# GLA's decay chain one head ahead, modulation summed by block transposes, and a phase's first projection made in the phase before

## The chip, the cores and the metric

One core of a Trainium2 chip runs the whole kernel. The metric is the device time of one execution in microseconds, as a median of several runs. Engine names: PE is the matrix engine (TensorE), PEld its weight loads, DVE the vector engine, ACT the scalar engine, POOL the GpSimd engine, SP the sync engine, which here only starts DMAs. Each engine works through its own program in order; semaphores join them.

## The reference

One inference step of a two-layer streaming encoder on 512 prompt frames and 64 sample frames of width 1024. Layer 0 runs mLSTM and retention heads side by side, layer 1 gated linear attention (GLA) and gated DeltaNet. Input and output of a layer are modulated by vectors made from a condition c (adaLN): `silu(c) @ w_ada + b_ada`, a sum over 1024 rows. Cut to what the change touches:

```python
log_a = jax.nn.log_sigmoid(a1.astype(F32) @ w_a2 + b_a2) / C_TAU       # GLA: decay input, rank 16
b = jnp.cumsum(_to_chunks(log_a, cs), axis=3)
q_t = qc * jnp.exp(b)
k_t = kc * jnp.exp(-b)
s = jnp.where(causal, jnp.einsum('nbhtd,nbhsd->nbhts', q_t, k_t), 0.0)
S = a_c[..., None] * S + jnp.einsum('bhsd,bhsv->bhdv', k_c, v_c)       # state, chunk by chunk
o = jnp.concatenate([_head_rmsnorm(hc), _head_rmsnorm(hd)], axis=-1) * g_head
```

## The kernel before

The phases follow one another, each a block of five engine programs that ends with a barrier: mLSTM, retention, output of layer 0, GLA, DeltaNet, output of layer 1. The function `heads(nc, M, IN, OUT, kind)` (from line 839) builds the first three of the four head phases: kind A is mLSTM, B retention, C GLA, each with H = 4 heads. Activations stay on chip transposed as a high and a low half of float32 (`hT_high`, `hT_low`); each product of a projection is three matmuls (`split_matmul`, lines 180 to 182).

A head (`turn(h, ...)` on each engine) has two parts. First the q and k projections: CT tiles of weights (4 in A and B, 2 in C), each in two halves of 288 tokens into PSUM banks 0 and 1, 24 matmuls a half, 48 a tile. ACT copies each half out (line 1204). Then five blocks t: four of 128 prompt tokens and one of 64 sample tokens. Per block PE makes the gates' projection into bank 2 (`project_gates`) and v's into bank 3 (`project_v`), 24 matmuls each, the scores and a transpose of k (bank 4), the products of scores and state with v (bank 6), the state update (banks 0 and 1), and transposes the gated result of the block before (`turn_g`, line 1080, bank 7), which DVE puts into `gT` (line 1481). In block 0 the gates come first, then v (in mLSTM v after the scores). ACT in block 0 does the tanh of the gates (1241), then the copy of v (1247) on which PE's product with the scores waits, then the copy of that product (1253).

The last block's `turn_g` of a head is done in the next head: in A and B behind the first weight tile, in C at once, behind the decay products. At the end of a phase it stands alone and everything waits for it.

Weights come by SP's DMAs, 512 KB a tile, into rings of two (`rqk`, `rv`); ACT rounds each to its high half (960, 973) and DVE makes the low half (967, 979). The first two q/k tiles of retention and GLA, and all four tiles of DeltaNet's first head, are loaded and split in the phase before (`FirstLoads`); the rest of such a head is requested when the phase begins.

GLA's decay chain stands at the head's start: PE multiplies the rank-16 input by `w_a2` (1092) into banks 0 and 1, ACT adds the bias (1198), DVE and ACT compute log-sigmoid (188 to 196), DVE scales and scans it (1357, 1360), takes the middle and end of each block (1366 to 1368), shifts (1371), ACT makes the exponentials (1208 to 1210) that multiply q and k (1375, 1379). PE's first q product waits for bank 0, that is for ACT's line 1198.

`LaterModulation` uses DVE's spare time in mLSTM and retention: `dve_step` k = 0 to 7 accumulates `w_ada` rows times silu(c) for two conditions (m) into `acc` [128, 2, 512] (line 667, two instructions a step), one step each in blocks 0 to 3 and four before them. Then `pe_total` (677), inside the `turn_g` of block 3, sums over the 128 partitions with eight matmuls against ones, and `dve_take` (689) copies eight columns.

## Time and profile before

| | us |
|---|---|
| median of 3 runs | 1641.48 |
| lowest, highest | 1640.67, 1643.29 |
| the profiled execution | 1638.62 |
| its span, first to last instruction | 1636.80 |
| mean granted clock of PE in it | 0.971 of full speed |

In a row of the timeline the bracket is the idle time of that engine just before the instruction, and what ended it. The granted clock (PEclk) is 1.00 at 2.4 GHz and 0.50 at 1.2 GHz; a stretch with 0.75 spent half its time at the lower level. The drawn end of a matmul is modelled and lies behind the time at which PE can take the next.

### The profile page before, as it was taken

The page shows a single profiled execution, that of the slowest core. Times are in us where ns is not written, and L with a number is a line of the kernel's source. Part 1 is how long each engine was busy: PE and PEld are TensorE (multiplying, and loading weights), DVE is VectorE, ACT ScalarE, POOL GpSimd, SP SyncE. Part 2 cuts the span into 40 slices and gives each one's busy share as a digit, 9 for nine tenths or more (in the row PEclk, how much of TensorE's full clock was granted, in tenths as well). Part 3 has the DMA queues.
Part 4 walks back from the last instruction along what each step waited for, and adds up shares of the span by engine and source line. Part 5 has one row for each costly group of instructions (what it writes and reads, how often), then busy time and mean ns, then how long its engine had stood idle before and what let it go on. Part 6 is the DMA issues. An engine that isn't in the chain of part 4 may idle for free. (4 is left out here: it accounts for less than half of the span.)

```text
span 1636.8 us, 30957 instructions
## 1 busy us (share of the span) xinstructions
PE 1529.1 (93%) x11168; PEld 1428.5 (87%) x11168; DVE 961.2 (59%) x2118; ACT 628.2 (38%) x1491; POOL 181.9 (11%) x384
## 2 busy tenths in 40 slices
PE   6999999998999999899799999899999999977898
PEld 2689898987999999899698889899999999966898
DVE  2575555554766667633566645576677667753522
ACT  2522222222232222423544433254555465543521
POOL 1000000000000000001000010023123222312000
PEclk8999999999999999999899999999999999988899
DMA  9434343432552433123343213221211211020223
GB/s 328 116 102 115 86 110 89 114 86 49 126 154 70 118 95 109 61 96 100 103 85 85 63 33 80 73 69 45 58 45 48 60 43 54 5 73 3 89 88 116
DMA packets 195257, 140.89 MB, mean 86 GB/s; under 512 B 18332, under 2 KB 178584, under 8 KB 194916
## 3 DMA queue, kind: packets, MB, share of 16 engines
q1 hardware_dynamic: 177772, 130.16, 28.2%
q10 hardware_dynamic: 17400, 9.60, 2.0%
q8 instruction: 53, 0.87, 0.2%
q14 instruction: 32, 0.26, 0.1%
HBM read 128.58 MB, written 11.15 MB: 85 GB/s over the span
## 5 line engine op out<-in xcount | busy, mean ns | idle before, releaser
L180 PE MATMUL bank<-hT,w_high 128*128 128x288 f32 x1152 | 363.0, 315 | 6.2 <-ACT gla_ls_x L1198 2.4
L182 PE MATMUL bank<-hT,w_high 128*128 128x288 f32 x1152 | 344.2, 299 | 0.0
L181 PE MATMUL bank<-hT,w_low 128*128 128x288 f32 x1152 | 344.2, 299 | 0.0
L180 PEld LDWEIGHTS bank<-hT,w_high 128*128 128x128 f32 x1152 | 222.1, 193 | 8.6 <-ACT gla_ls_x L1198 2.6
L181 PEld LDWEIGHTS bank<-hT,w_low 128*128 128x128 f32 x1152 | 222.0, 193 | 0.0
L182 PEld LDWEIGHTS bank<-hT,w_high 128*128 128x128 f32 x1152 | 221.2, 192 | 0.0
L180 PE MATMUL bank<-output_w_split,gT_high 128*128 128x256 f32 x512 | 143.4, 280 | 0.0
L182 PE MATMUL bank<-output_w_split,gT_high 128*128 128x256 f32 x512 | 143.2, 280 | 0.0
L181 PE MATMUL bank<-output_w_split,gT_low 128*128 128x256 f32 x512 | 142.5, 278 | 0.0
L181 PEld LDWEIGHTS bank<-output_w_split,gT_low 128*128 128x128 f32 x512 | 96.8, 189 | 0.0
L180 PEld LDWEIGHTS bank<-output_w_split,gT_high 128*128 128x128 f32 x512 | 96.1, 188 | 0.1
L182 PEld LDWEIGHTS bank<-output_w_split,gT_high 128*128 128x128 f32 x512 | 95.9, 187 | 0.0
L180 PE MATMUL bank<-mlstm_w_v_low,hT 128*128 128x512 f32 (+1 forms) x256 | 88.8, 347 | 0.0
L181 PE MATMUL bank<-mlstm_w_v_high,hT 128*128 128x512 f32 (+1 forms) x256 | 86.2, 337 | 0.0
L182 PE MATMUL bank<-mlstm_w_v_high,hT 128*128 128x512 f32 (+1 forms) x256 | 85.6, 334 | 0.0
L180 PE MATMUL bank<-gla_w_v_low,hT 128*128 128x256 f32 x256 | 74.0, 289 | 0.0
L180 PE MATMUL bank<-retention_w_v_low,hT 128*128 128x256 f32 x256 | 73.5, 287 | 0.0
L181 PE MATMUL bank<-gla_w_v_high,hT 128*128 128x256 f32 x256 | 71.5, 279 | 0.0
L182 PE MATMUL bank<-gla_w_v_high,hT 128*128 128x256 f32 x256 | 71.4, 279 | 0.0
L182 PE MATMUL bank<-retention_w_v_high,hT 128*128 128x256 f32 x256 | 71.4, 279 | 0.0
L181 PE MATMUL bank<-retention_w_v_high,hT 128*128 128x256 f32 x256 | 71.4, 279 | 0.0
L2123 POOL TENSOR_TENSOR gdn_A_level<-gdn_AT,const 128x128 f32<-128x128 f32 (+1 forms) x120 | 61.0, 542 | 76.7 <-DVE gdn_AT L2038 68.1
(487 smaller groups left out, 3594.4 us busy)
## 6 DMA issues: line engine op xcount, KB each, us to landing
x<-in_w_in_even SPq DMA_DIRECT2D x72, 512.0 KB, 5.0
x<-in_w_in_odd SPq DMA_DIRECT2D x56, 512.0 KB, 4.3
x<-in_w_ada SPq DMA_DIRECT2D x32, 256.0 KB, 4.2
front_w_ada<-in_w_ada SPq DMA_DIRECT2D x6, 1024.0 KB, 15.1
output_w_raw<-in_w_out_even SPq DMA_DIRECT2D x12, 512.0 KB, 3.4
output_w_raw<-in_w_out_odd SPq DMA_DIRECT2D x12, 512.0 KB, 3.4
gdn_E<-G_rows SPq DMA_DIRECT2D x8, 576.0 KB, 4.9
gT<-in_w_ada SPq DMA_DIRECT2D x16, 256.0 KB, 4.1
```

The lines of the kernel that those rows point to most:

```text
L180: pe.matmul(out, w[0], x[1], start=first, stop=False)
L181: pe.matmul(out, w[1], x[0], start=False, stop=False)
L182: return pe.matmul(out, w[0], x[0], start=False, stop=last)
L2123: last = pool.tensor_tensor(tiles(ML[:, n % 2, :], t), tiles(AT, t), lev[0:R, 0:R], ALU.mult)
```

## The change

- **Decay chain a head ahead (GLA).** PE makes the decay products of head h+1 in head h's block 0, behind the scores. Its links on DVE and ACT go to blocks 0 to 3 of head h. Only head 0 has the chain at its start. Block 3's factors for the state (`eend`) are made at the next head's start. The copies of block middles and ends are joined (6 instructions in place of 15). The gate chain of DeltaNet moves: its scan and ends to blocks 0 and 1 of head 1, its columns into block 3 of head 1.
- **Order and banks.** The q/k projections go to banks 3 and 2 (A, B) or 1 and 5 (C). The last `turn_g` of a head stands behind the next head's first tile in all kinds. v's weights are loaded and projected before the gates' in every block, and in C the ring for them has three places.
- **Modulation.** DVE transposes `acc` in 32x32 blocks and sums over 32, in block 3; PE makes one matmul of 32 columns against a folding matrix; DVE takes the result in four copies. The step of block 3 moves ahead of it: to block 0 (A), before the second rotation (B).
- **First projection ahead.** At the end of mLSTM and GLA, before the last `turn_g`, PE makes the 48 products of the next phase's first tile.

```diff
+    def dve_fold(self, dve, h):
+
+        dve.wait_ge(*self.summed.done(h, 2 * KT - 1))
+        blocks = self.more.rearrange("p m c -> p (m c)")
+        dve.transpose(blocks, self.acc.rearrange("p m c -> p (m c)")).then_inc(self.folded.sem, 1)
+        dve.wait_ge(*self.folded.done(h, 0))
+        dve.wait_ge(*self.total_psum.before(h, 0))
+        dve.tensor_reduce(self.part[:], blocks.rearrange("p (b r) -> p b r", r=QUAD), AX.X, ALU.add).then_inc(self.folded.sem, 1)
...
     def pe_total(self, pe, h):
-        M = self.M
-        pe.wait_ge(*self.summed.done(h, 2 * KT - 1))
+        M, n = self.M, 2 * 512 // QUAD
+        if self.kind == "A" and isinstance(h, int) and h == 0:
+            pe.wait_ge(*self.rest.done(0, 15))
+        pe.wait_ge(*self.folded.done(h, 1))
         pe.wait_ge(*self.total.before(h, 0))
-        for c in range(4):
-            for m in range(2):
-                at = 256 + 2 * c + m
-                last = pe.matmul(M["ps"][7][:, at:at + P], self.acc[:, m, c * P:(c + 1) * P], M.c("ones")[:, 0:P], start=True, stop=True)
-        last.then_inc(self.total_psum.sem, 1)
...
+        pe.matmul(M["ps"][7][:, 2 * P:2 * P + n], M.c("fold"), self.part[:], start=True, stop=True).then_inc(self.total_psum.sem, 1)
...
+        for j in range(P // QUAD):
+            at = slice(j * QUAD, (j + 1) * QUAD)
+            src = M["ps"][7][at, 2 * P:2 * P + n].rearrange("p (m c j) -> p c m j", m=2, j=P // QUAD)[:, :, :, j:j + 1]
+            last = dve.tensor_copy(out[at].rearrange("p a c m -> p (a c) m"), src.rearrange("p c m j -> p c (m j)"))
+        last.then_inc(self.total.sem, 1)
...
+    PROJ = (1, 5) if kind == "C" else (3, 2)
+    VS = 3 if kind == "C" else 2
...
-        after = {"A": (0, 2, 2, 4, 4, 6), "B": (0, 2, 4, 6), "C": (1, 2, 3, 4)}[kind]
+        after = {"A": (0, 2, 2, 4, 4, 6), "B": (0, 2, 4, 6), "C": (-1, -1, 0, 1)}[kind]
...
-                    c0 = (gates0 + [v0])[c // 2] + c % 2 * P
-                    sp.wait_ge(*(v_low.done(h, c - 2) if c >= 2 else v_low.before(h, 0)))
-                    sp.dma_start(rv[:, c % 2], w_in[:, :, bass.ds(h * DV + c0, P)]).then_inc(wvl[c % 2].sem, 16)
+                    c0 = ([v0] + gates0)[c // 2] + c % 2 * P
+                    sp.wait_ge(*(v_low.done(h, c - VS) if c >= VS else v_low.before(h, 0)))
+                    sp.dma_start(rv[:, c % VS], w_in[:, :, bass.ds(h * DV + c0, P)]).then_inc(wvl[c % VS].sem, 16)
...
-                    if kind == "C":
-                        sp.wait_ge(*qk_psum.before(h, 0))
-                        sp.dma_start(wa[:], IN["w_a2"][0][:, bass.ds(h * P, P)]).then_inc(wal.sem, 16)
+                    if kind == "C" and ahead is not None:
+                        sp.wait_ge(*ls_psum.done(h, 1))
+                        sp.dma_start(wa[:], IN["w_a2"][0][:, bass.ds(ahead * P, P)]).then_inc(wal.sem, 16)
...
+                def turn(h, previous, ahead=None):
+
+                    def project_decay(h):
                         pe.wait_ge(*wal.done(h, 15))
+                        pe.sem_inc(M.passed, 1)
                         for n in range(2):
-                        if previous is not None:
-                            turn_g(previous, T - 1)
+                            pe.matmul(PS[PROJ[n]][:, 0:HALF], wa[:], M["a1T"][0:RANK, n * HALF:(n + 1) * HALF],
+                                      start=True, stop=True).then_inc(ls_psum.sem, 1)
+
+                    if kind == "C" and previous is None:
+                        project_decay(h)
                     for ct in range(CT):
                         pe.wait_ge(*qk_low.done(h, ct))
+                        if kind == "B" and previous is None and ct == 0:
+                            pe.wait_ge(M.first_psum, 2)
+                            pe.sem_inc(qk_psum.sem, 2)
+                            continue
                         if kind == "A" and previous is None and ct == 0:
-                            front.pe_projections(pe, (qkh[:, 0], qkl[:, 0]), qk_psum)
+                            front.pe_projections(pe, (qkh[:, 0], qkl[:, 0]), qk_psum, PROJ)
                             continue
+                        if kind == "C" and (previous, ct) == (1, 0):
+                            pe.wait_ge(chain.step.sem, 4)
                         for half in range(2):
-                            n = NA + 2 * ct + half
-                            pe.wait_ge(*(qk_copied.done(h, n - 2) if n >= 2 else qk_copied.before(h, 0)))
+                            n = 2 * ct + half
+                            pe.wait_ge(*(qk_copied.done(h, n - 2) if n >= 2 else ls_copied.done(h, n) if kind == "C" else
+                                         (v_copied, gates_used)[half].before(h, 0)))
                             to = slice(half * HALF, (half + 1) * HALF)
                             for k in range(KT):
...
                         if t == 0:
-                            pe.wait_ge(*v_low.done(h, NG // P - 1))
+                            pe.wait_ge(*v_low.done(h, DV // P - 1))
+                            if kind != "C":
+                                pe.wait_ge(*qk_copied.done(h, NP - 2))
+                        if t != 1 or kind != "B":
+                            project_v(t)
                         if t == 0:
-                            project_gates(t)
-                            pe.wait_ge(*v_low.done(h, NC - 1))
                             if kind != "A":
-                                project_v(t)
+                                pe.wait_ge(*v_low.done(h, NC - 1))
+                            if kind == "B":
+                                pe.wait_ge(*qk_copied.done(h, NP - 1))
+                                project_gates(t)
...
+                if kind in "AC":
+                    pe.wait_ge(*first.low.done(0, 0))
+                    for half, bank, free in (((0, 3, v_copied), (1, 2, gates_used)) if kind == "A" else ((1, 1, v_copied), (0, 0, nS_ready))):
+                        pe.wait_ge(*free.done(H - 1, T - 1))
+                        to = slice(half * HALF, (half + 1) * HALF)
+                        for k in range(KT):
+                            last = split_matmul(pe, PS[bank][:, 0:HALF], (qkh[:, 0, k, :], qkl[:, 0, k, :]),
+                                                (M["hT_high"][:, k, to], M["hT_low"][:, k, to]), k == 0, k == KT - 1)
+                        last.then_inc(M.first_psum, 1)
                 turn_g(H - 1, T - 1)
...
+                def take_decay(h):
+                    for n in range(2):
+                        act.wait_ge(*ls_psum.done(h, n))
+                        act.sem_inc(M.passed, 1)
+                        act.activation(la[:, n * HALF:(n + 1) * HALF], PS[PROJ[n]][:, 0:HALF], ACT.Identity,
+                                       bias=M["vec"][:, bass.ds(h + 64, 1)]).then_inc(ls_copied.sem, 1)
+
...
+                def block_factors(h):
+                    act.wait_ge(*shifted.done(h, 0))
+                    act.wait_ge(*state_ready.before(h, 0))
+                    act.activation(eend[:], ends[:], ACT.Exp).then_inc(eend_ready.sem, 1)
...
                         if t == 0:
                             tanh_gates()
+                            if kind == "C" and ahead is not None:
+                                take_decay(ahead)
                         act.wait_ge(*v_psum.done(h, t))
                         act.wait_ge(*state_psum.before(h, t))
                         act.activation((v_sample if t == PT else v)[0:R, 0:DV], PS[3][P - R if t == PT else 0:P, 0:DV], ACT.Copy
                                        ).then_inc(v_half.sem if t == PT else v_copied.sem, 1)
+                        if kind == "C" and ahead is not None and t in (0, 1):
+                            (decay_exp, decay_log)[t](ahead)
...
+                        if kind == "C" and ahead is not None and t == PT - 1:
+                            decay_factors(ahead)
...
-                        if later and t and t < PT:
+                        if later and t in (1, 2):
                             later_step(h)
+                        if later and t == PT - 1:
+                            later.dve_fold(dve, h)
+                        if kind == "C" and t == 0:
+                            dve.wait_ge(*eend_ready.done(h, 0))
+                        if kind == "C" and ahead is not None:
+                            if t == 0:
+                                decay_abs(ahead)
+                            elif t == 1:
+                                decay_log(ahead, link)
+                            elif t == 2:
+                                decay_sums(ahead, link)
+                            elif t == 3:
+                                decay_shift(ahead, link)
+                        if kind == "C" and t == PT - 1 and isinstance(h, int) and h == 1:
+                            chain.dve_columns(dve)
...
+                        if kind == "C" and t == 0 and ahead is not None:
+                            decay_plus(ahead)
...
-                project(pe, 0, 0, 8 * KT)
+                pe.wait_ge(M.first_psum, 4)
+                pe.wait_ge(*s["proj_copied"].before(0, 0))
+                pe.sem_inc(s["proj_psum"].sem, 2)
+                project(pe, 0, 2 * KT, 8 * KT)
```

## Rows read from the trace of the kernel before

**Rows 1.** The page, busy time of each engine, its share of the span, instructions.

```profile
PE 1529.1 (93%) x11168; PEld 1428.5 (87%) x11168; DVE 961.2 (59%) x2118; ACT 628.2 (38%) x1491; POOL 181.9 (11%) x384
```

**Rows 2.** Busy time in a stretch (GLA): length, PE, PEld, DVE, ACT, POOL, PEclk, DMA, GB/s.

```profile
812.00:1031.00 219.00, 204.49 (x1516) 195.85 (x1514) 127.58 (x357) 93.45 (x186) 17.90 (x40) 0.95 0.29 68
```

**Rows 3.** What PE waited for, whole span: total us, times, longest.

```profile
PE bank L1080 <- DVE gT L1481: 12.1, 6, 3.8
PE bank L173 <- ACT mlstm_v L1247: 3.6, 4, 1.9
PE bank L173 <- DVE gla_scores L1392: 2.6, 4, 0.7
```

**Rows 4.** Timeline, GLA head 0 into head 1: start, length, engine, line, operation [idle before].

```profile
863.07 0.38 PE L1080 MATMUL bank<-const,gla_g 128*128 128x128 f32 x2
863.81 1.23 PE L1092 MATMUL bank<-gates,gla_w_a 16*128 16x288 f32 x4 [0.35 <-DVE gla_state_new L1432]
864.77 0.89 ACT L1198 ACTIVATE gla_ls_x<-bank,vectors 128x288 f32<-128x288 f32 x2 [1.01 <-PE bank L1092]
866.13 0.46 PE L1080 MATMUL bank<-const,gla_g 66*128 66x66 f32 x2 [1.09 <-DVE gT L1481]
```

**Rows 5.** Stretches of 48 projection products in GLA: columns as in Rows 2.

```profile
866.34:875.47 9.13, 9.13 (x50) 9.13 (x50) 5.44 (x10) 4.96 (x6) 0.00 (x0) 0.67 0.16 41
875.47:881.83 6.36, 6.36 (x50) 6.36 (x49) 4.60 (x27) 4.40 (x8) 0.00 (x0) 1.00 0.99 262
923.50:931.48 7.98, 7.97 (x48) 7.98 (x49) 4.99 (x7) 5.32 (x7) 0.00 (x0) 0.78 0.08 17
977.09:985.05 7.96, 7.96 (x49) 7.96 (x49) 5.28 (x9) 4.96 (x6) 0.00 (x0) 0.79 0.06 11
```

**Rows 6.** Timeline, PE, last transposes of GLA heads 1 and 2.

```profile
917.06 0.38 PE L1080 MATMUL bank<-const,gla_g 128*128 128x128 f32 x2
...
973.21 0.39 PE L1080 MATMUL bank<-const,gla_g 128*128 128x128 f32 x2
```

**Rows 7.** Timeline, block 0 of an mLSTM head: the copy of v.

```profile
183.79 0.38 ACT L1247 ACTIVATE mlstm_v<-bank 128x256 f32<-128x256 f32 x1 [2.89 <-PE bank L182]
184.32 0.67 PE L173 MATMUL bank<-mlstm_v,mlstm_scores 128*128 128x257 f32 x2 [0.56 <-ACT mlstm_v L1247]
```

**Rows 8.** The tanh of the gates, durations ns min/median/max.

```profile
L1241 ACT ACTIVATE mlstm_tanh<-bank x16: 579/598/598, 101.0 to 380.8; 128x512 f32<-128x512 f32 x16
...
L1241 ACT ACTIVATE gla_tanh<-bank x16: 384/384/386, 828.6 to 1020.2; 128x256 f32<-128x256 f32 x16
```

**Rows 9.** Timeline, GLA head 0, block 4.

```profile
861.75 0.62 PE L173 MATMUL bank<-gla_v_sample,gla_scores 66*66 66x256 f32 x2 [1.07 <-DVE gla_v_sample L1408]
```

**Rows 10.** Timeline, PE, GLA into DeltaNet.

```profile
1026.79 0.39 PE L1080 MATMUL bank<-const,gla_g 128*128 128x128 f32 x2
1030.34 0.45 PE L1080 MATMUL bank<-const,gla_g 66*128 66x66 f32 x2 [3.16 <-DVE gT L1481]
1032.24 0.61 PE L180 MATMUL bank<-hT,w_high 128*128 128x288 f32 x1 [1.45 <-DVEq L2196]
```

**Rows 11.** Stretch of 48 products at the start of retention.

```profile
399.07:408.06 8.99, 8.99 (x48) 8.99 (x49) 0.20 (x2) 1.07 (x2) 0.00 (x0) 0.69 0.69 127
```

**Rows 12.** DMA issues at retention's start: KB each, median us to landing.

```profile
x<-in_w_in_even SPq DMA_DIRECT2D x3, 512.0 KB, 10.9
```

**Rows 13.** Timeline, PE, modulation sums of mLSTM's last head.

```profile
391.46 1.95 PE L677 MATMUL bank<-const,gT 128*128 128x128 f32 x16
```

**Rows 14.** Groups of DVE instructions in retention: busy us, mean ns.

```profile
L667 DVE SCALAR_TENSOR_TENSOR retention_later_sum<-retention_later_ring,silu_c,retention_later_sum 128x512 f32<-128x512 f32 x32 | 22.5, 744 | 0.0
L979 DVE TENSOR_TENSOR retention_w_v_low<-x,retention_w_v_high 128x1024 fp32r<-128x1024 f32 x16 | 19.6, 1225 | 15.4 <-ACT retention_w_v_high L973 14.7 <-issue 0.5
```

**Rows 15.** Groups of DVE instructions in DeltaNet: busy us, mean ns.

```profile
L1997 DVE TENSOR_REDUCE gdn_ss<-gdn_tanh_conv 128x10 f32<-128x1280 f32 x8 | 11.9, 1487 | 2.9 <-ACT gdn_tanh_conv L1896 2.9
```

**Rows 16.** Stretch behind mLSTM head 0's block 0: columns as in Rows 2.

```profile
102.00:109.00 7.00, 7.00 (x46) 6.45 (x47) 4.82 (x15) 1.48 (x5) 0.74 (x2) 1.00 0.03 11
```

More of the change, by code:

```diff
@@ L43 @@
 EVEN_H, GLA_H, GDN_H = 4, 4, 8
+QUAD = 32
 RANK = 16
@@ L415, in pe_projections @@
                 g = split_matmul(pe, PS[5 + half][0:36, 0:HALF], (self.wgh[:, k, :], self.wgl[:, k, :]), x, first, last)
-                q = split_matmul(pe, PS[half][:, 0:HALF], (w[0][:, k, :], w[1][:, k, :]), x, first, last)
+                q = split_matmul(pe, PS[banks[half]][:, 0:HALF], (w[0][:, k, :], w[1][:, k, :]), x, first, last)
                 if last:
@@ L1362, in turn @@
-                        link(last)
-                        for t in range(T):
-                            mid = t * P + rows(t) // 2 - 1
-                            end = t * P + rows(t) - 1
-                            dve.tensor_copy(ends[:, 0, t:t + 1], bT[:, mid:mid + 1])
-                            dve.tensor_copy(ends[:, 2, t:t + 1], bT[:, end:end + 1])
-                            last = dve.tensor_scalar(ends[:, 1, t:t + 1], bT[:, end:end + 1], bT[:, mid:mid + 1], None, ALU.subtract)
```

231 lines of the change are left out of this document (138 added, 93 removed).

## The prediction

> **What bounds the kernel now.** I read the page's table of engines first: the matrix engine (PE) is busy 93% of the span and no other engine more than 59% [rows 1]. A change can therefore gain in three ways only: fewer columns through PE, less idle time on PE, or fewer stretches at half clock. The table of stretches shows where there is room: in the GLA phase PE is busy 204.5 of 219.0 us at a mean clock of 0.95 [rows 2]. The list of PE's waits names the causes: it waits for the vector engine (DVE) to have put away the last transposed block of a head (12.1 us in six waits), for the scalar engine's (ACT) copy of v in mLSTM (3.6 us), and for the masked scores in GLA (2.6 us) [rows 3]. In the timeline of a GLA head's start PE has its last product at 863.07, does the decay products at 863.81, idles 1.09 us and comes to the 48 projection products at 866.34 [rows 4]. These 48 take 9.13 us, the next 48 take 6.36, since the clock falls to its lower level behind the idle time [rows 5].
>
> **The sum is made against the profiled run**, 1638.62 us for a span of 1636.8. The median of the runs is 1641.48, 2.9 us more. I subtract the difference from the median.
>
> **GLA head starts (heads 1 to 3).** The decay chain moves into the head before, and the last transpose of a head moves behind 48 products. From a head's last transposes to the end of the first 48 it is now 875.47 - 863.07 = 12.40, 931.48 - 917.06 = 14.42 and 985.05 - 973.21 = 11.84 us [rows 4 to 6]. Afterwards I count 0.22 (two transposes) + 6.36 (48 at full clock) + 0.3 (last transpose) = 6.9 us. The decay products (about 1.0 us of PE) and, in the second, the gate columns (about 1.1 us) are moved, not removed. Gain: 12.40 - 7.9 = 4.5, 14.42 - 9.0 = 5.4, 11.84 - 7.9 = 3.9, together **13.8 us**. That holds if the chain is done in time. Its links go to DVE in blocks 0 to 3 of the head before, one each, in front of the gating. PE is with a gate projection then (24 products, 2.8 us) and no link is longer than 1.6 us, so I cost them at nothing; without that cover each would cost its length, up to 6 us a head.
>
> **GLA block 0.** This is what takes back most. Projections of v now come first and the gates second, but ACT's program still does the tanh of the gates, then (new) two copies of the next head's decay input, and only then the copy of v on which PE's next product waits. What a copy of v costs PE mLSTM shows: 0.56 us idle behind a product's modelled end [rows 7], 0.17 more since such a product is drawn 0.28 long where the next could start after 0.12, so 0.73, of which 0.38 is the copy and 0.35 the releases. In GLA PE so waits 0.35 + 0.38 (tanh [rows 8]) + 0.89 (two copies [rows 4]) + 0.38 (copy of v [rows 7]) + 0.05 (issue) = 2.05 us. It has 0.8 us of idle there now (four waits for the scores, 0.6 each by the list [rows 3]). Loss: 1.25 in heads 0 to 2, and 0.3 in head 3, which has no head ahead. In head 0 the chain isn't ahead, its cover shrinks by one projection of 2.8 us, and sync (SP) now holds the first v weights back until the decay products are done. I take 1.0 us more there; the ends are 0 and 3. Loss: 3 x 1.25 + 0.3 + 1.0 = **5.1 us**.
>
> **Other GLA edits.** A scan of gate rows leaves head 0's block 3, where PE waits 1.07 us for what is queued behind it [rows 9]: gain **1.1 us**. The joined copies of block ends save only DVE time that PE doesn't wait for. The columns moved into head 1's block 3 cost nothing new.
>
> **GLA into DeltaNet.** It now takes 1032.24 - 1026.79 = 5.45 us to the first product, 3.2 of it idle and 1.9 the phase change (from 1030.34) [rows 10]; then 48 products partly at half clock, 8.2 us (between the 7.96 and 9.13 of [rows 5]): 13.6 us. Afterwards: 0.22 + 6.36 products, 1.9 phase change, and 0.5 since the next product waits for ACT to copy the one done ahead = 9.0. Gain **4.6 us**. All four weight tiles of DeltaNet's first head are loaded ahead already, so nothing is late there.
>
> **mLSTM into retention.** The same move: 3.8 us of idle [rows 3] and 8.99 - 6.36 = 2.6 us of half clock [rows 5, 11] could go. I expect nothing of it. The first retention head loads v and the third q/k tile only when the phase begins, and such a load of 512 KB takes 10.9 us to land [rows 12], while DMA moves only 127 GB/s at 0.69 busy [rows 11]: small state stores are in its way. What PE does ahead brings it to the third tile when that isn't there. ACT's queue is in order as well: q/k copy, split of v (waits for its load), then the second q/k copy, for which PE's bank waits. So PE idles 7 us in another place, the clock falls once more, and the third tile starts at about 414.7 in place of 414.4. I count a loss of **0.4 us**; the ends are 1.5 gained and 3 lost.
>
> **Modulation sums.** The eight products (16 records) take 1.95 us per head by the row, of which 0.2 is the last one's drain, so 1.74 [rows 13]; one product with 32 columns stays, 0.2 us by the nearest short rows. It counts where PE is the limit: three heads of mLSTM and three of retention. The last head of each is followed by idle time, or is in the sum above. Gain 6 x 1.54 = **9.2 us**. DVE pays with a block transpose and a reduction over 1024 columns in block 3, in place of one step (2 x 0.744 [rows 14]). The reduction is 1.487 x 1024/1280 = 1.2 us [rows 15]. The transpose is in no row; the nearest pass of 128x1024 takes 1.225 [rows 14], and I take that; the ends are 0.7 (faster than any such pass here) and 4.9 (four passes). Together 2.5 us against 1.5. In retention the scores of block 4 are needed about 10.8 us of PE work after those of block 3, and DVE's other work between, with its waits for ACT and POOL, is about 6.2: 4.6 us of slack. Free, then. At 4.9 the fold would be 6.1 us and cost 1.5 us in four heads. The result is taken in four small copies in place of one, 0.3 us at the end of retention: loss **0.3 us**. The vector page of the Trainium skill ("Vector Engine (DVE) Microarchitecture Reference", 3.8) has a transpose stream one element per cycle and lane, which is the plain pass that I took; no run so far shows it.
>
> **mLSTM and retention, block 0.** In mLSTM v now comes before the gates, again with ACT's tanh in front of the copy of v. PE waits 0.73 + 0.6 (tanh of 512 columns [rows 8]) + 0.03 = 1.36 us against 0.73 now [rows 7]. In head 0 another wait covers both. Loss 3 x 0.63 = **1.9 us**. In retention a sum step moves in front of the second rotation: 0.2 us in four heads, **0.8 us**. The other banks for the q/k products change whom the first product of a head waits for; all of those are done at that time, and PE doesn't idle at these boundaries now.
>
> **Sum.** 13.8 + 1.1 + 4.6 + 9.2 = 28.7 gained; 5.1 + 0.4 + 0.3 + 1.9 + 0.8 = 8.5 lost; net 20.2. 1641.5 - 20.2 = **1621.3 us**.
>
> **The rivals.** (a) Forecast, 0.50, own range 1616 to 1627. (b) **The hand-over into retention pays.** If the loads of that phase land as much earlier as PE is ahead, it gains 3.8 + 2.6 = 6.4 in place of losing 0.4: 1614.5. For it: PE's idle and slow time there is real. Against: the load that takes 10.9 us. 0.15. (c) **The clock falls again in GLA's block 0**, and so in three heads: a fallen stretch costs 9.13 - 6.36, or 1.6 in the milder two [rows 5], about 2.2 each, 6.6 together: 1627.9. Against: mLSTM's first head has a wait of 2.1 us before 102 and full clock behind it [rows 16]; for: the decay products with 16 rows and the wait stand close together. 0.18. The skill's "TensorE: Matmul & The Clock Gate" ("A second HAM failure mode") has short idles between groups of products, often repeated, bring the low clock back; by it this case would be the likely one. (d) **The change doesn't do what it says**: the chain isn't ahead because a link waits in DVE's or ACT's order and ends behind the next head's first projections. Then half of the 13.8 is left: 1628.2. 0.05. (e) **DVE gives time back in the fold**, at the upper end: 4 x 1.5 = 6 us: 1627.3. 0.08. (f) **Slower than before**: the same fold as a mechanism with a threshold. DVE works in order, so blocks 4 of retention wait for it beyond 4.6 us and those of mLSTM beyond about 8.5 us (block longer by 3.9). To lose 20.2 + 3.3 us over four heads of each it must take F with 4(F - 4.6) + 4(F - 8.5) = 23.5, F = 9.5 us, a transpose of 8.3 us, seven plain passes. Then 1644.8 or more. 0.02. The remaining 0.02 lies about no change.
>
> **How the numbers follow.** Likeliest is (a): 1621.3. The range takes in (b), (c), (d) and (e) with the bounds of head 0, of retention's start and of the fold: 1611 to 1632. A measurement of this kernel tells about 0.2% from no change, that is 1638.2 to 1644.8. Faster 0.95, same 0.03, slower 0.02.
>
> **What the profile after would show.** GLA starts: no wait between a head's last product and its first projections, and 48 of these in 6.4 us. Block 0: a wait of 2.0 us on the copy of v in three GLA heads, of 1.4 in mLSTM. Retention's start: PE idle 5 us or more in the first head, with ACT waiting for loads, and a clock below 0.8. Fold: a transpose of about 1.2 us on DVE, no waits of PE for it. Wrong is the forecast if block 0 shows no wait (then 5 to 7 us faster), if clock rows of GLA stay at 0.95, or if retention's first head has no idle time.

## The result, and the profile after

| | before | changed |
|---|---|---|
| median, us (8 runs each, taking turns) | 1643.85 | 1633.26 |
| range of the runs, us | 1640.67 to 1649.05 | 1628.94 to 1637.26 |
| profiled execution, us (its span) | 1638.62 (1636.8) | 1632.42 (1630.7) |
| mean granted clock in it | 0.971 | 0.974 |

The ratio is 0.9933, with a 95% interval of 0.9917 to 0.9948: 11 us gained (8.5 to 13.6), where 20.2 were forecast. In a later set the same kernel came to 0.9918 (0.9902 to 0.9934), 13 us. The changed kernel is faster, but by little more than half the forecast. The kernel before took 2.4 us more in this comparison than in the three runs (1641.48) that the forecast started from, so the gain is the figure to go by.

The page of the changed kernel begins like this (the line of [rows 1], then the clock by slice):

```profile
PE 1520.0 (93%) x11056; PEld 1419.0 (87%) x11056; DVE 979.9 (60%) x2122; ACT 625.5 (38%) x1491; POOL 181.0 (11%) x384
...
PEclk9999999999999999899899999999999999988999
```

PE has 9.1 us less work than in [rows 1], and the span is 6.1 us shorter. So PE idles 3 us more than before, although GLA's head starts no longer make it wait. The rows of mLSTM (56 to 396) and retention (396 to 672) in the kernel before, then the same of the changed kernel and below them the stretch of [rows 2]; columns as in [rows 2]:

```profile
56.00:396.00 340.00, 331.94 (x2141) 302.46 (x2141) 201.25 (x462) 105.66 (x214) 16.51 (x42) 1.00 0.35 97
396.00:672.00 276.00, 273.24 (x2070) 266.34 (x2071) 178.36 (x336) 76.29 (x165) 14.06 (x38) 0.99 0.40 106
```

```profile
56.00:396.00 340.00, 328.64 (x2082) 298.67 (x2083) 209.31 (x469) 104.30 (x211) 15.23 (x40) 0.99 0.35 94
396.00:672.00 276.00, 268.96 (x2011) 261.10 (x2011) 190.52 (x361) 75.64 (x166) 14.73 (x40) 0.98 0.40 107
812.00:1031.00 219.00, 209.52 (x1568) 200.24 (x1568) 125.69 (x327) 94.76 (x189) 18.32 (x40) 0.98 0.30 71
```

In GLA PE is now busy 209.5 of 219.0 us at a clock of 0.98, against 204.5 at 0.95. That part came as forecast. In the two phases above it PE is idle longer than before, and the clock is a little lower. The list of what PE waited for, in mLSTM and in the first retention head, shows where it was lost (total us, times, longest):

```profile
PE bank L182 <- ACT retention_qkT_raw L1273: 6.9, 2, 4.8
PE bank L182 <- ACT gT L1273: 6.1, 3, 2.6
PE bank L175 <- ACT mlstm_v L1316: 5.2, 4, 2.1
```

The wait for the last transposed block at mLSTM's end has gone from the list of [rows 3]. Two others are new. One was foreseen, in retention's first head (6.9 us). The other was not: three waits of 6.1 us in heads 1 to 3 of mLSTM. L182 is a projection of q and k; it waits until ACT has put away the product two before it (L1273). ACT's timeline in head 1 says why that comes late (start, length, engine, line, operation [idle time before it and what ended it]):

```profile
149.56 0.49 ACTq L1350 DMA_DIRECT2D out_sn<-state  x1
...
156.56 1.05 ACT L982 ACTIVATE mlstm_w_v_high<-x 128x1024 fp32r<-128x1024 f32 x1
163.17 1.06 ACT L982 ACTIVATE mlstm_w_v_high<-x 128x1024 fp32r<-128x1024 f32 x1 [5.56 <-DMA x<-in_w_in_even]
164.13 0.39 ACT L1273 ACTIVATE gT<-bank 128x288 f32<-128x288 f32 x1
```

ACT stands 5.56 us at the split of the third v/gate tile, whose load hasn't landed, and the copy for which PE waits is queued behind it. The two kernels' DMA issues in this stretch, before (149 to 157.5) and changed (149 to 156), with KB each and us from issue to landing:

```profile
x<-in_w_in_even SPq DMA_DIRECT2D x1, 512.0 KB, 6.1
out_sC<-state ACTq DMA_DIRECT2D x1, 256.0 KB, 5.7
out_sn<-state ACTq DMA_DIRECT2D x1, 1.0 KB, 11.0
```

```profile
x<-in_w_in_even SPq DMA_DIRECT2D x1, 512.0 KB, 8.3
out_sC<-state ACTq DMA_DIRECT2D x1, 256.0 KB, 5.8
out_sn<-state ACTq DMA_DIRECT2D x1, 1.0 KB, 9.3
```

The load is the same, and it is issued 1.84 us earlier (154.82 against 156.66), but lands no earlier: 163.15 against 162.79. What is odd in the table is the store of 1 KB that takes 9 to 11 us. It is the n column of the state, 256 pieces of 4 bytes (the second such store of a head: one for the prompt state, one for the sample state), issued by ACT at 149.4 to 149.6 in both kernels.

**Where the time went, stretch by stretch.** Marks are the starts of the last state update of each head, from the timelines. Us in the kernel before; then the difference by the prediction's terms and in two profiled runs of the changed kernel:

| stretch | before | forecast | changed | again |
|---|---|---|---|---|
| start to mLSTM's first state update | 102.5 | 0 | -1.4 | -1.2 |
| rest of mLSTM head 0 | 42.4 | 0 | +1.6 | 0.0 |
| mLSTM heads 1 to 3 | 245.5 | -2.7 | +4.1 | +2.7 |
| to the end of retention head 0 | 76.0 | +0.6 | +1.6 | +1.0 |
| retention heads 1 to 3 | 203.1 | -4.0 | -3.5 | -3.5 |
| to GLA's first state update | 163.4 | +3.6 | +6.6 | +3.6 |
| rest of GLA | 193.5 | -13.1 | -11.9 | -12.1 |
| from there to the end | 610.5 | -4.6 | -3.2 | -2.7 |
| span | 1636.8 | -20.2 | -6.1 | -12.2 |

The column "forecast" holds the terms of the sum, each put where its time falls (a decay product moved from a head's start into the block 0 before is counted there). The first profile has 4.6 us more than the second in two stretches (mLSTM head 0, and up to GLA's first state update), and most variants below don't show them either. What stays is that mLSTM's heads 1 to 3 are 5.4 to 6.8 us off, and in the second run no other stretch is off by more than 2. Two variants of the second set (without the hand-over, and with the orders of GLA's first head put back) leave mLSTM's own instructions as they are; there the three heads take 244.2 and 246.6 us, 1.4 and 3.8 off. So the size of this loss changes from one execution to the next, from 1.4 to 6.8 us in four profiles.

### The profile page after: what moved, and what is told of

Read it like the earlier page. It is cut to its first block and busy times, and to the rows that moved or that the text cites. A ratio compares the mean times of both kernels' runs of the same rounds, so it can differ in the third digit from the quotient of the medians.

```text
span 1630.7 us, 30733 instructions
## 1 busy us (share of the span) xinstructions
PE 1520.0 (93%) x11056; PEld 1419.0 (87%) x11056; DVE 979.9 (60%) x2122; ACT 625.5 (38%) x1491; POOL 181.0 (11%) x384
## 5 line engine op out<-in xcount | busy, mean ns | idle before, releaser
L182 PE MATMUL bank<-hT,w_high 128*128 128x288 f32 x1152 | 362.1, 314 | 15.0 <-ACT retention_qkT_raw L1273 6.9
L182 PEld LDWEIGHTS bank<-hT,w_high 128*128 128x128 f32 x1152 | 220.6, 191 | 17.4 <-ACT gT L1273 6.8
L182 PE MATMUL bank<-output_w_split,gT_high 128*128 128x256 f32 x512 | 143.7, 281 | 0.0
L182 PEld LDWEIGHTS bank<-output_w_split,gT_high 128*128 128x128 f32 x512 | 96.1, 188 | 0.1
L182 PE MATMUL bank<-mlstm_w_v_low,hT 128*128 128x256 f32 (+1 forms) x256 | 89.9, 351 | 0.0
L184 PE MATMUL bank<-mlstm_w_v_high,hT 128*128 128x256 f32 (+1 forms) x256 | 86.7, 339 | 0.0
L183 PE MATMUL bank<-mlstm_w_v_high,hT 128*128 128x256 f32 (+1 forms) x256 | 86.5, 338 | 0.0
L182 PE MATMUL bank<-gla_w_v_low,hT 128*128 128x256 f32 x256 | 75.1, 293 | 0.0
L182 PE MATMUL bank<-retention_w_v_low,hT 128*128 128x256 f32 x256 | 73.7, 288 | 0.1
L184 PE MATMUL bank<-retention_w_v_high,hT 128*128 128x256 f32 x256 | 71.5, 279 | 0.0
L2242 POOL TENSOR_TENSOR gdn_A_level<-gdn_AT,const 128x128 f32<-128x128 f32 (+1 forms) x120 | 60.5, 536 | 76.8 <-DVE gdn_AT L2157 68.1
## 6 DMA issues: line engine op xcount, KB each, us to landing
front_w_ada<-in_w_ada SPq DMA_DIRECT2D x6, 1024.0 KB, 13.9
```

The lines of the kernel that those rows point to most:

```text
L182: pe.matmul(out, w[0], x[1], start=first, stop=False)
L183: pe.matmul(out, w[1], x[0], start=False, stop=False)
L184: return pe.matmul(out, w[0], x[0], start=False, stop=last)
L2242: last = pool.tensor_tensor(tiles(ML[:, n % 2, :], t), tiles(AT, t), lev[0:R, 0:R], ALU.mult)
```

## The experiments

Each set ran beside the kernel before on one chip; ratios are to it, with 95% intervals. Kernels of different sets are compared by their ratios; the changed kernel is 0.9918 (last set) and 0.9933 (first measurement).

**First set: what holds the load up?** The theory: the small stores of the n column. They follow a head's end by a fixed time, the load lands 13 to 14 us after the second, and what PE gains between them is waited away. The rival: the load is slow or late by itself.

```
-  act.dma_start(n_out, St[i][:, :, DV:NV], allow_slow_non_contiguous=True).then_inc(st, 16)
+  act.sem_inc(st, 16)
```

> The changed kernel, with the two stores of the state's extra column per mLSTM head left out (prompt and sample state n; each is 256 pieces of 4 bytes, and these outputs are not written). In the changed kernel the matrix engine waits 2.2, 2.8 and 1.7 us in heads 1 to 3 of mLSTM, before the second half of the third q/k tile. Theory 1: the load of the third v/gate tile is held up by these stores. It lands 13 to 14 us after the second of them was issued, in both kernels, whether the load itself was issued at 156.7 or at 154.8. Without them it lands some 5 us after its own issue, the three waits go (6.6 us, and 1.7 of half clock behind one of them), and at retention's start most of the 7.3 us of idle time goes too: 1619 to 1626 us, ratio to before 0.985 to 0.989. Theory 2: the load is just slow or issued late (its place comes free late), and the stores have no part in it: within 1.5 us of the changed kernel, 1632 to 1635, ratio 0.993.

Measured: 1616.18 us against 1638.1, ratio 0.9869 (0.9851 to 0.9886). The load, now issued at 155.4, lands in 3.7 us, and the three waits are gone:

```profile
x<-in_w_in_even SPq DMA_DIRECT2D x1, 512.0 KB, 3.7
```

```profile
PE bank L175 <- ACT mlstm_v L1316: 5.5, 4, 2.3
PE bank L182 <- ACT retention_qkT_raw L1273: 3.2, 2, 2.1
```

The heads take 80.2, 80.3 and 80.2 us, where the changed kernel took 82.7, 84.8 and 82.1. The way to the end of retention's head 0 is 71.8 us, 5.8 shorter; with the idle time go 10.2 us of half clock that the changed kernel has there, in two stretches. The same edit in the kernel before:

> The kernel before, with the same stores of the n column left out. Theory 1 (the stores hold the loads up, but the matrix engine of this kernel comes late enough not to feel it): 0.4 us in each of three heads and about 1 us at retention's start, in all 1 to 3 us faster than before, ratio 0.998 to 0.9995, so that the two changes together are worth more than each alone. Theory 2 (the stores have no part): ratio 0.999 to 1.001. If it gains 6 us or more, the stores cost the kernel before as much as the changed one, and they don't explain the missing gain.

Measured: ratio 0.9988 (0.9978 to 0.9998), 2.0 us. The stores cost the kernel before 2 us and the changed one 8 to 10.5 (0.9869 against 0.9918 to 0.9933). So they are a limit that the kernel before barely touched, and that the change ran into. Then the same wait from the other side, by ACT's order:

```
-  after = {"A": (0, 2, 2, 4, 4, 6), ...
+  after = {"A": (0, 2, 3, 4, 4, 6), ...
   # on DVE: low_qk (n in 1, 3) ahead of low_v, for kind A
```

> The changed kernel, with the split of the third v/gate tile of an mLSTM head (which waits for its load) moved on ACT and DVE behind the copy of the q/k product and behind the split of the fourth q/k tile, for both of which the matrix engine waits. Theory A: what the matrix engine waits for at these three places is ACT's queue, in which the copy stands behind the split that waits for the load, and nothing needs the split itself that early. The three waits go, 5 to 8 us with the stretch at half clock: 1625 to 1629, ratio 0.988 to 0.991. Theory B: the loads themselves are the limit: the later tiles of the gates come later by as much, and the wait comes back in block 0 in front of the gates: 1632 to 1635, ratio 0.993.

Measured: 1623.82 us, ratio 0.992 (0.9905 to 0.9935), no clear gain beside the changed kernel's 0.9918 and 0.9933. Three waits of 3.9 us in all are left, in place of 6.1 and 5.0 in the two profiles of the changed kernel. The wait comes back one tile later, at the next load (247.97 in head 2):

```profile
243.54 1.06 ACT L982 ACTIVATE mlstm_w_v_high<-x 128x1024 fp32r<-128x1024 f32 x1 [0.36 <-DMA x<-in_w_in_even]
248.02 1.06 ACT L982 ACTIVATE mlstm_w_v_high<-x 128x1024 fp32r<-128x1024 f32 x1 [3.42 <-DMA x<-in_w_in_even]
248.98 0.69 ACT L1273 ACTIVATE gT<-bank 128x288 f32<-128x288 f32 x2
```

Theory B, then: the loads are the limit, and the order in ACT's queue only says at which product it is felt. I had thought that the wait would come back in the gates; it came back at the last half of q and k. Last in this set, the sums:

```
   in pe_total:
-  pe.wait_ge(*self.folded.done(h, 1))
-  pe.matmul(M["ps"][7][:, 2 * P:2 * P + n], M.c("fold"), self.part[:], start=True, stop=True)
+  pe.wait_ge(*self.summed.done(h, 2 * KT - 1))
+  for c in range(4):
+      for m in range(2):
+          ... self.acc[:, m, c * P:(c + 1) * P], M.c("ones")[:, 0:P] ...
   # dve_fold gone, dve_take one copy as before
```

> The changed kernel with the modulation sums made as in the kernel before (eight products with ones, no block transpose, no reduction), all else as changed. By the prediction the sums are worth 1.54 us in six heads: this kernel would be 9.2 us slower than the changed one, 1642 to 1643, ratio 0.999. By the theory that mLSTM's heads are tied to the landing of a load, which comes a fixed time after the stores at the head's start and not after the matrix engine's products, the 1.5 us are given back in each of heads 1 to 3 of mLSTM, and the sums are worth 3 x 1.28 in retention alone, or less than nothing in mLSTM if the wait brings half clock (1.7 us after one wait in the profile): 0 to 4.5 us slower than the changed one, 1633 to 1638, ratio 0.9935 to 0.996.

Measured: 1628.45 us, ratio 0.9941 (0.9925 to 0.9957). With the old sums the kernel is 1 to 4 us slower, not 9. In retention a head takes 68.1 us with them and 66.5 without, as forecast. In mLSTM the three heads take 81.9, 81.9 and 82.0, in all 245.8, which lies within what they take with the new sums (244.2 to 249.6 in the four profiles): PE comes 1.6 us later to the third tile and has nothing to wait for. The list holds no wait for `gT` L1272 any more:

```profile
PE bank L182 <- ACT retention_qkT_raw L1272: 6.8, 2, 4.7
PE bank L175 <- ACT mlstm_v L1315: 4.8, 4, 1.6
```

**Second set: block 0, the hand-over, another form of the store, GLA's first head.**

```
   if t == 0:                      # moved behind the copy of v
       tanh_gates()
       if kind == "C" and ahead is not None:
           take_decay(ahead)
```

> The changed kernel with ACT's order in block 0 turned round: it copies v first, and does the tanh of the gates and (in GLA) the two copies of the next head's decay input after it. Theory A (as in the prediction): the matrix engine's wait in block 0 is the sum of what stands ahead of the copy in ACT's queue. It falls from 1.74 to about 0.5 in three GLA heads and from 1.21 to about 0.6 in heads 1 to 3 of mLSTM, and nothing else comes late: 5 to 5.5 us faster than the changed kernel, ratio to before 0.990. Theory B: tanh or the decay copies are needed as urgently (the gated z, or the chain for the next head), and the wait appears a few products later: within 1 us of the changed kernel, ratio 0.993.

Measured: 1613.37 us against 1638.9, ratio 0.9842 (0.9827 to 0.9856). That is more than expected. By stretch, GLA's three gaps between heads shrink (last state update of one to the first of the next) from 23.1, 23.1 and 22.1 to 21.3, 21.3 and 21.1 us, and retention's heads by 0.3 each (66.5 to 66.2). mLSTM's heads 1 to 3 take 241.8 us. That is 2.4 to 7.8 less than in the four profiles with the old order, where 1.8 was expected; waits for the late load are left there (4.2 us), but no stretch of half clock, which both profiles of the changed kernel have in these heads (1.7 us each). How much of the surplus is the order, and how much the chance of the load, isn't shown. ACT's queue in GLA's block 0, changed kernel and then this one:

```profile
891.55 0.38 ACT L1308 ACTIVATE gla_tanh<-bank 128x256 f32<-128x256 f32 x1 [6.19 <-PE bank L184]
891.83 0.88 ACT L1237 ACTIVATE gla_ls_x<-bank,vectors 128x288 f32<-128x288 f32 x2
892.60 0.39 ACT L1316 ACTIVATE gla_v<-bank 128x256 f32<-128x256 f32 x1
```

```profile
871.66 0.39 ACT L1312 ACTIVATE gla_v<-bank 128x256 f32<-128x256 f32 x1 [2.10 <-PE bank L184]
876.15 0.38 ACT L1308 ACTIVATE gla_tanh<-bank 128x256 f32<-128x256 f32 x1 [4.11 <-PE bank L184]
876.43 0.89 ACT L1237 ACTIVATE gla_ls_x<-bank,vectors 128x288 f32<-128x288 f32 x2
```

The copy of v stood behind tanh and the decay copies, which wait for the gates; v's own product had long been there. Put first, it is done 4 us before the tanh. Next, the hand-over:

```
-  if kind in "AC":
+  if kind == "C":
       pe.wait_ge(*first.low.done(0, 0))
   # and kind B makes its first projection itself again
```

> The changed kernel without the hand-over from mLSTM to retention: retention makes its first q/k projection itself, as before; the hand-over from GLA to DeltaNet stays. Theory A: the first loads of retention land 12.5 to 14 us after the last store of the n column, whatever the matrix engine has done ahead, and the hand-over only moves its idle time there: it is worth nothing or costs 1 to 1.5 us, ratio 0.992 to 0.9935. Theory B (the rival of the prediction): the hand-over pays, 3.8 us of idle and 2.6 of half clock: this kernel is 4 to 6.4 us slower than the changed one, ratio 0.996 to 0.997.

Measured: 1622.82 us, ratio 0.9908 (0.9891 to 0.9925). Not slower than the changed kernel: the way from mLSTM's end to that of retention's head 0 is 77.2 us, against 77.6 and 77.0 with the hand-over. It is worth nothing there, as the prediction had it. Now the store in a form that keeps the outputs whole:

```
+  dve.transpose(nt[i][:].rearrange("p (d c) -> p d c", d=DT), St[i][:, :, NV - QUAD // DT:NV])
-  act.dma_start(n_out, St[i][:, :, DV:NV], allow_slow_non_contiguous=True).then_inc(st, 16)
+  for d in range(DT):
+      act.dma_start(n_out[d], nt[i][QUAD // DT * (d + 1) - 1:P:QUAD, :]).then_inc(st, 16)
```

> The changed kernel with the n column stored in another form, outputs complete: DVE turns the last 16 columns of both halves of the state in 32x32 blocks (one instruction per store, behind the gated h, where it waits anyway), and ACT stores each half as 4 pieces of 128 bytes in place of 128 pieces of 4 bytes. Theory 1: what holds the loads up is the number of 4-byte pieces. Then this is as fast as the kernel without these stores, up to 1 us for two more DMA issues on ACT per store: ratio 0.987 to 0.988. Theory 2: it is the stores as such (their order in the queue behind the big state stores, or the queue's latency): the waits of 1.7 to 2.8 us stay, ratio 0.992 to 0.993.

Measured: 1613.3 us, ratio 0.9853 (0.9833 to 0.9873). It does as much as leaving the stores out. The turn costs DVE 200 ns each time, and the load lands in 3.8 us:

```profile
L1595 DVE STREAM_TRANSPOSE n_rows<-state 128x32 f32<-128x32 f32 x8 | 1.6, 200 | 0.0
```

```profile
x<-in_w_in_even SPq DMA_DIRECT2D x1, 512.0 KB, 3.8
```

```profile
PE bank L182 <- ACT retention_qkT_raw L1275: 3.0, 2, 2.1
```

The stores stand where they stood: the last is issued at 148.3, and the load at 153.0, 4.7 us behind it (5.3 in the changed kernel). So it is the form of the store, 256 pieces of 4 bytes against 8 of 128. Whether their number or their smallness does it isn't told apart. Last, GLA's first head:

```
   # DVE, head 0: decay_log, decay_sums, decay_shift ahead of low_v(0), low_v(1)
   # SP: load_v(0), load_v(1) ahead of the wait for ls_psum and the load of wa
```

> The changed kernel with two orders in GLA's first head put back: DVE goes through the decay chain before it splits v's first two tiles, and SP issues the loads of v before it waits for the decay products. Theory A: the head's 5.3 us of extra length up to its first state update (1.2 of them are the next head's decay products) are partly the late load of v (it lands at 819.8 in place of 815.5) and the chain queued behind its split: the wait of 1.05 us for the scaled k goes, and the half-clock stretch behind it (1.7 us) perhaps too: 1 to 3 us faster than the changed kernel, ratio 0.9915 to 0.993. Theory B: the loads of v land late because of other transfers, and the splits then come too late for the matrix engine: no gain or 1 us slower, ratio 0.993 to 0.994.

Measured: 1622.3 us, ratio 0.9891 (0.9875 to 0.9906). The ratio lies below what either theory said, but the gain is not in the place in question: to GLA's first state update it takes 167.6 us, 167.0 without the edit. The order of that head isn't where time was lost; why the median came out lower isn't shown (its interval overlaps that of the changed kernel's 0.9918).

**Third set: the changed kernel again, and the remedies with and without the parts of the change.**

> The changed kernel once more, as it is, so that the three others of this set stand beside it on the same chip. The first time it was 0.9933 of before; the parts measured since stand for a sum nearer to 0.990. Its profile had in mLSTM's first head and ahead of GLA's first state update 1.6 and 3.3 us more than six and eight of the variants, which have the same code there. If that was chance of that run, these two stretches are 42.4 and 166.6 us long this time (44.0 and 170.0 then), and the ratio is 0.990 to 0.993.

Measured: 1625.26 us against 1637.47, ratio 0.9918 (0.9902 to 0.9934). Both stretches came out as most variants had them, 42.4 and 167.0 us.

> Both remedies in one: the n column turned and stored in 128-byte pieces, and v copied first in block 0 by ACT. Each alone gave about 0.985 of before. By the theory that one acts on the stretch between a head's stores and the third q/k tile and the other in block 0, their gains add up in GLA (1.8 + 1.8 + 1.0 us there) and in block 0 of mLSTM (0.6 in each of three heads) and retention (0.3 each): 6 to 8 us faster than the rows alone, 1605 to 1608, ratio 0.979 to 0.981. If the gain of the one was the same microseconds as the gain of the other (both reach the same limit by the loads), it stays at 0.984 to 0.985.

Measured: 1604.06 us, ratio 0.9797 (0.9782 to 0.9813), 33 us faster than the kernel before and 21 faster than the changed one (1625.26). The gains add up for the most part: beside 0.9918, v first alone is worth 12.4 us, the rows alone 10.6 and both together 19.8. mLSTM's heads take 79.1, 79.0 and 78.9 us, and GLA runs at full clock from the first state update of head 0 on:

```profile
815.70:1006.00 190.30, 185.16 (x1431) 178.27 (x1430) 111.70 (x304) 82.83 (x173) 18.51 (x41) 1.00 0.25 64
```

```profile
PE bank L182 <- ACT retention_qkT_raw L1275: 2.1, 1, 2.1
PE bank L175 <- DVE mlstm_scores L1505: 1.0, 1, 1.0
```

Then the two by two for the sums and for the hand-over:

> The n column in rows, and the modulation sums made the old way: with the changed kernel, the one with old sums and the one with rows this makes two by two. By the theory that the sums' gain in mLSTM is given back at the load which the 4-byte pieces hold up, it comes out in full here: this kernel is 6 x 1.5 = 9 us slower than the one with rows (three heads of mLSTM and three of retention), ratio 0.990 to 0.991, whereas with the pieces the difference of old and new sums was 1 to 2 us. If the sums are not worth their 1.54 us in mLSTM for a reason of their own (DVE's fold delaying block 3 or 4), it is 4 to 5 us slower, ratio 0.988.

Measured: 1622.68 us, ratio 0.9911 (0.9896 to 0.9925). Beside 0.9853 that is 9.5 us for the sums. mLSTM's heads 1 to 3 take 245.5 us with old sums and 240.8 with new ones, retention's 204.3 and 199.5: 1.5 and 1.6 us a head.

> The n column in rows, and no hand-over from mLSTM to retention. Theory: the hand-over is good and was only made worthless by the late loads. From mLSTM's last state update to the last of retention's first head it takes 71.5 us with rows and the hand-over, and 75.3 in the kernel before without the n stores. This kernel should take about 75, so 3 to 5 us slower than the one with rows: ratio 0.9875 to 0.989. If the rows alone brought the 4.6 us that this stretch gained, it stays at 0.985.

Measured: 1616.57 us, ratio 0.9869 (0.9855 to 0.9884), against 0.9853. The stretch itself takes 75.9 us against 71.5 with the hand-over, 4.4 us; by the ratios it is 2.6, with intervals that overlap. By the stretch, the hand-over pays once the loads come in time; in the whole time it isn't clear of the noise.

## Why the prediction was wrong

The direction was right, the size was not: 1621.3 forecast, 1633.26 measured, outside the range's upper end of 1632.

**The step that failed** is in the part on the modulation sums: "It counts where PE is the limit: three heads of mLSTM and three of retention." In retention that held: the sums give 1.57 us a head there, of which block 0 takes back 0.4 (0.2 forecast). In mLSTM PE was the limit only just. The waits of the kernel before had it: two waits of 0.7 us together, in head 1, on the same copy, and in ACT's timeline of heads 2 and 3 the load ends the idle time ahead of it (first row: PE's waits from 150 to 175; then ACT in head 2):

```profile
PE bank L180 <- ACT gT L1204: 0.7, 2, 0.4
```

```profile
245.19 1.06 ACT L973 ACTIVATE mlstm_w_v_high<-x 128x1024 fp32r<-128x1024 f32 x1 [3.64 <-DMA x<-in_w_in_even]
246.16 0.39 ACT L1204 ACTIVATE gT<-bank 128x288 f32<-128x288 f32 x1
```

PE's products start 0.13 us apart; the last of the first half starts at 246.23, and the first of the second half only at 246.60, behind the end of the copy at 246.55. So it is 0.24 us late, too little to show in the list. By the same reckoning it is 0.4 late in head 1 (164.23 after 163.70), and in head 3 on time (328.06 after 327.91). There was no margin in any of the three heads. I had not looked for a margin there, since almost no wait showed. A second chain runs beside PE's there, from the last state update through the store of the n column to the load of the third v/gate tile, and it doesn't pass through the sums. PE came 1.5 us earlier to a load that did not, and waited: the load took up to 2.6 us longer from its issue to its landing (8.4 against 5.8 us in head 2). The wait brought a stretch of half clock there, 3.4 us from 248.4. In the two profiles of the changed kernel mLSTM's heads 1 to 3 so became 2.7 and 4.1 us longer in place of 2.7 shorter: the 4.6 us of the sums were lost, and 0.8 to 2.2 more. In the two variants with the same mLSTM they became 1.3 shorter and 1.1 longer. With the store in rows the 4.6 us are there (245.5 against 240.8), so the price of the sums was right and their place was not.

That is 5.4 of the 8 us that the second profile is short of the forecast. The largest of the rest is the change into DeltaNet (1.9), then a wait in GLA's head 3 (1.0); both are below.

I had named this very mechanism at the start of retention, where I wrote that small state stores stand in the way of the loads. I took it for a matter of the phase change and didn't ask where else a head's loads follow its stores.

The other steps:

- **GLA head starts**: right in the main. No wait is left between a head's last product and its first projections, and the 48 products take 6.57, 6.56 and 6.53 us at full clock (forecast 6.4):

```profile
870.90:877.47 6.57, 6.57 (x54) 6.57 (x52) 2.30 (x6) 4.29 (x9) 0.99 (x2) 1.00 0.06 21
923.28:929.84 6.56, 6.56 (x53) 6.56 (x52) 2.30 (x6) 4.55 (x10) 0.99 (x2) 1.00 0.06 21
974.08:980.61 6.53, 6.53 (x53) 6.53 (x52) 2.29 (x6) 4.28 (x9) 0.99 (x2) 1.00 0.06 20
1032.66:1039.50 6.84, 6.84 (x40) 6.84 (x41) 5.59 (x13) 1.57 (x4) 0.11 (x1) 0.75 0.93 230
```

  One wait was put at nothing: in head 3 PE now waits 1.0 us ahead of v's first projection, since DVE has not split v's weights in time:

```profile
PE bank L175 <- DVE gla_w_v_low L990: 1.0, 1, 1.0
```

- **Block 0**: right in kind and about in size. In three GLA heads PE idles 1.57 us by the rows, 1.74 with the 0.17 that the prediction adds for the drawn end (2.05 forecast), and in mLSTM 1.05, so 1.2 (1.36). The experiment that turned ACT's order gave back 1.8, 1.8 and 1.1 us in GLA's heads 1 to 3. That is more than the 1.25 and 0.3 that I charged, as a part of the 0.8 of wait that was there before goes too.
- **GLA head 0**: 3.6 us longer up to the first state update in the second run and 3.1 to 3.3 in most variants, 3.6 forecast. The 6.6 of the first profile hold a wait (0.9) and a stretch of half clock (from 835.5) that the second run doesn't have.
- **GLA into DeltaNet**: 2.7 to 3.2 us in place of 4.6. The fourth row above shows it: behind the phase change the clock falls for 3.4 us (0.75 over these 6.84 us). That costs 1.7 us, and I had the products there at full clock. The term was too big, the move right.
- **mLSTM into retention**: right that it gives nothing. PE idles 2.1 and 4.8 us in the first head, the third tile starts at 414.4 (414.7 forecast), the clock is 0.76 from 399 to 420 (below 0.8 forecast), ACT waits for the load of v, and the copy is queued behind that:

```profile
399.14 0.49 ACTq L1350 DMA_DIRECT2D out_sn<-state  x1
...
413.02 1.06 ACT L982 ACTIVATE retention_w_v_high<-x 128x1024 fp32r<-128x1024 f32 x1 [8.45 <-DMA x<-in_w_in_even]
413.98 0.39 ACT L1273 ACTIVATE retention_qkT_raw<-bank 128x288 f32<-128x288 f32 x1
```

  The load lands 13.9 us after the store of the n column at 399.14. The stretch became 1.0 to 1.6 us longer, but without the hand-over it is 1.2 longer too, so the hand-over itself is worth between 0.2 gained and 0.4 lost.
- **The fold**: right. No wait of PE for it, and its two steps cost what the plain pass of [rows 14] and the reduction of [rows 15] said, 1.23 and 1.22 us:

```profile
L663 DVE STREAM_TRANSPOSE gT<-gT 128x1024 f32<-128x1024 f32 x4 | 4.9, 1233 | 0.0
...
L666 DVE TENSOR_REDUCE mlstm_later_part<-gT 128x32 f32<-128x1024 f32 x4 | 4.9, 1220 | 0.1
```

  The statement of the Trainium skill that I had quoted ("Vector Engine (DVE) Microarchitecture Reference", 3.8) agrees with this: the turn costs what a plain pass of that size costs.
- **Rivals**: (c), the clock falling again in GLA's heads 1 to 3, did not happen: 0.98 in GLA, and the waits on the copy of v brought no half clock there in any profile. It did happen behind waits of mLSTM. (b) came true only with the stores in rows, and then with 2.6 to 4.4 us of its 6.4; that kernel is 24 us faster than the one before. (d), (e) and (f) are out. The true case was none of them.

## What to carry to other kernels

Before counting a gain on the busiest engine, ask by how much each thing that it needs next is early: an input that comes just when it is used shows no wait, and a gain in front of it can be worth nothing all the same. Follow each load back to what stands ahead of it in the transfers, small stores first, since here a store of 1 KB held up a load of 512 KB. And in an engine's queue put the copy whose input is ready ahead of those that still wait.

## What was not expected of the hardware

- A store of 256 pieces of 4 bytes (1 KB) took 7.7 to 11.7 us to land in the two kernels, where in mLSTM 256 KB in pieces of 1 KB took 2.6 to 7.9. A load of 512 KB issued 5 to 7 us behind it, by another engine and on another queue, landed in 5.8 to 8.4 us, and without it or with 128-byte pieces in 3.6 to 3.8. In the changed kernel the transfers stand nearly still between the two:

```profile
150.00:152.00 2.00, 2.00 (x17) 2.00 (x16) 1.24 (x6) 1.36 (x2) 0.57 (x2) 1.00 0.46 132
152.00:155.00 3.00, 3.00 (x26) 3.00 (x24) 2.38 (x6) 1.36 (x2) 0.00 (x0) 1.00 0.00 0
155.00:158.00 3.00, 3.00 (x25) 3.00 (x24) 1.93 (x4) 1.36 (x2) 0.00 (x0) 1.00 0.23 10
158.00:160.00 2.00, 2.00 (x17) 2.00 (x16) 0.87 (x1) 0.00 (x0) 0.00 (x0) 1.00 0.32 42
160.00:162.00 2.00, 2.00 (x17) 2.00 (x16) 0.00 (x0) 0.00 (x0) 0.00 (x0) 1.00 0.77 184
```

  The last columns are the transfers' busy share and GB/s: 10 and 42 GB/s in the 5 us behind the load's issue at 154.8, and then 184. With the store in rows they are at 112 GB/s in the first 2 us behind the issue (153 to 155). The Trainium skill has two sentences that bear on this: transfers of different engines end up on the same 16 engines ("DMA: Bandwidth & Descriptors", Issuing engines are not separate DMA queues), and the semaphore's update waits for the writes ahead of it to be confirmed, which "can cause a surprisingly long delay", above all with a target in HBM ("Perfetto Trace Analysis", DMA Instruction — HWDGE). That a store of ACT holds up a load of SP agrees with the first. The second fits the long landing of the small stores, but which step of a transfer is held up the runs don't show.
- Whether the clock falls behind a short wait changes from one execution to the next. In mLSTM's head 0 the changed kernel idled 2.1 us by the rows and then ran 3.4 us at half clock (from 101.6); a wait of 2.0 us in its head 1 (to 164.6) brought none. In its second profile a wait of 1.7 us in head 3 brought half clock, and three of 1.5 to 1.6 us didn't. The kernel before idled 1.9 us in head 0 and kept full clock. The 1.6 us that this costs is as much as one of the effects looked for, so such a term should be read from more than one profile.
